# Sparse attention visits its sixteen token tiles alternately, most keys and fewest keys, instead of in rising order

## The reference, cut to what matters

```
# per block of 128 query tokens (start = 128 * t)
rel = relu(einsum('bqhd,bsd->bqhs', q_idx, k_idx)); score = einsum('bqhs,bqh->bqs', rel, w_idx)
score = where(key_pos <= qpos, score, -inf)
_, sel = top_k(score, 256)                      # an indexer picks 256 keys per query
kg, vg = gather(k, sel), gather(v, sel)
sc = einsum('bqkgd,bqjkd->bqkgj', qg, kg) * scale   # 8 heads, 2 key-value groups, head dim 64
p = softmax(where(valid, sc, -inf)); o = einsum('bqkgj,bqjkd->bqkgd', p, vg)
```

## Time and profile before

| what | value |
|---|---|
| median of 3 runs | 3377.59 us (3375.81 to 3380.34) |
| the profiled execution, its own time | 3379.56 us |
| its span (first to last instruction) | 3377.7 us, mean granted clock 0.97 |
| busy share of the span | PE 93%, PEld 78%, DVE 62%, ACT 54%, POOL 23% |
| sparse attention within the span | 1603.3 to about 2070 us |

### The profile page before, as it was taken

The page is one execution under the profiler, slowest core; times in us unless marked ns, Lnnn a source line. Parts: engine busy times, 40 slices in busy tenths (PEclk is TensorE's granted clock), DMA queues, the critical chain, the costliest instruction groups (busy, mean ns, idle before and its releaser), DMA issues. The chain is left out here.

```text
span 3377.7 us, 51228 instructions
## 1 busy us (share of the span) xinstructions
PE 3145.0 (93%) x17304; PEld 2641.0 (78%) x17304; DVE 2081.9 (62%) x5122; ACT 1822.9 (54%) x3613; POOL 776.7 (23%) x1078
## 2 busy tenths in 40 slices
PE   7999879999979999997899997999989999869998
PEld 5888768888868777776667776999878888769997
DVE  5767668888845666564899886534446666632112
ACT  5565556676756766663777774211246666632121
POOL 6444411011012122232211001101034444311110
PEclk8999989999989999998899998999999999979999
DMA  4666664436152222225511103544432222244332
GB/s 172 201 200 200 201 137 90 95 71 142 57 196 78 75 86 78 82 79 125 138 43 31 31 20 99 175 132 132 167 124 69 74 74 56 62 144 127 124 125 75
DMA packets 307188, 370.46 MB, mean 110 GB/s; under 512 B 24800, under 2 KB 251936, under 8 KB 303088
## 3 DMA queue, kind: packets, MB, share of 16 engines
q1 hardware_dynamic: 293728, 320.77, 32.7%
q0 software_dynamic: 13200, 46.42, 4.3%
HBM read 216.32 MB, written 150.80 MB: 109 GB/s over the span
## 5 line engine op out<-in xcount | busy, mean ns | idle before, releaser
L93 PE MATMUL i_p_g<-i_hT_lo,i_wh 128*128 128x512 f32 x768 | 308.2, 401 | 9.3 <-DVE i_wl L1639 9.3
L95 PE MATMUL i_p_g<-i_hT_hi,i_wh 128*128 128x512 f32 x768 | 306.0, 398 | 0.0
L94 PE MATMUL i_p_g<-i_hT_hi,i_wl 128*128 128x512 f32 x768 | 306.0, 398 | 0.0
L1657 DVE SCALAR_TENSOR_TENSOR i_score<-i_relu,i_w,i_score 128x1024 f32<-128x1024 f32 (+7 forms) x154 | 155.2, 1024 | 166.6 <-ACT i_relu L1542 164.7
L1552 ACT ACTIVATE i_above<-i_score,i_less 128x2048 bf16<-128x2048 f32 (+13 forms) x140 | 183.1, 1308 | 104.5 <-POOL i_less L1609 67.6
L1081 DVE TENSOR_TENSOR mla_tl<-mla_p_t,mla_th 128x512 fp32r<-128x512 f32 (+1 forms) x320 | 186.1, 606 | 45.3 <-ACT mla_th L1124 41.8
L1124 ACT ACTIVATE mla_th<-mla_p_t 128x512 fp32r<-128x512 f32 (+1 forms) x320 | 163.9, 530 | 86.4 <-PE mla_p_t L1021 83.8
L1081 DVE TENSOR_TENSOR dsa_tl<-dsa_p_t,dsa_th 128x512 fp32r<-128x512 f32 x272 | 180.0, 686 | 42.8 <-ACT dsa_th L1124 36.6
L1051 DVE CUSTOM_DVE_ANT_0 dsa_probs<-dsa_p_s,dsa_mask 128x512 f32<-128x512 f32 (+3 forms) x320 | 184.6, 605 | 16.0 <-PE dsa_p_s L1806 14.5
L1124 ACT ACTIVATE dsa_th<-dsa_p_t 128x512 fp32r<-128x512 f32 x272 | 155.4, 593 | 70.4 <-PE dsa_p_t L1021 69.7
L1542 ACT ACTIVATE i_relu<-i_p_s 128x1024 f32<-128x1024 f32 (+7 forms) x176 | 141.6, 813 | 77.8 <-DVE i_score L1654 39.4
(11 more groups left out here) (337 smaller groups left out, 9667.9 us busy)
## 6 DMA issues: line engine op xcount, KB each, us to landing
scratch_gates<-i_ob SPq DMA_DIRECT2D x95, 256.0 KB, 2.4
m_m<-scratch_gates SPq DMA_DIRECT2D x64, 256.0 KB, 4.0
f_hs<-scratch_h2T SPq DMA_DIRECT2D x16, 1024.0 KB, 9.9
scratch_qkT<-b_th SPq DMA_DIRECT2D x64, 192.0 KB, 2.6
scratch_qkT<-b_tl SPq DMA_DIRECT2D x64, 192.0 KB, 2.9
i_ws<-in_w_in SPq DMA_DIRECT2D x24, 512.0 KB, 4.4
b_xt<-in_x SPq DMA_DIRECT2D x16, 512.0 KB, 4.8
scratch_h<-b_xh POOLq DMA_DIRECT2D x16, 512.0 KB, 3.0
```

The lines of the kernel that those rows point to most:

```text
L93: pe.matmul(out, l[0], r[1], start=start, stop=False)
L94: pe.matmul(out, l[1], r[0], start=False, stop=False)
L95: return pe.matmul(out, l[0], r[0], start=False, stop=stop)
L1657: nc.vector.scalar_tensor_tensor(out=acc, in0=r, scalar=w[:, t, h:h + 1], in1=acc, op0=ALU.mult, op1=ALU.add).then_inc(summed, 1)
```

## The change

A list `order` of tiles replaces the rising order: 0, 1, 15, 2, 14, 3, 13, 4, 12, 5, 11, 6, 10, 7, 9, 8. Buffers, waits and loads now count places in this list (x), and tiles (t) only where the data are addressed. The wait for the second piece of keys and values moves to the third place, since tile 15 stands there. Every unit keeps its own work; what changes is which unit's blocks stand beside which unit's scores. The loops (k, k) for k = 1 to 16 and (2, 1) stay. The fourteen loops (k+1, k) for k = 2 to 15 go; in their place come seven loops of **many scores beside few blocks**, (16, 2), (15, 3), (14, 4), (13, 5), (12, 6), (11, 7), (10, 8), and seven of **few scores beside many blocks**, (3, 16), (4, 15), (5, 14), (6, 13), (7, 12), (8, 11), (9, 10). The blocks that stand alone at the end are those of tile 8, nine instead of 16.

```diff
+        few, many = list(range(2, NT // 2 + 1)), list(range(NT - 1, NT // 2, -1))
+        self.order = [0, 1] + [t for pair in zip(many, few) for t in pair]
         self.units = [dict(keys=[P * (t + 1)] * 4, blocks=[(j, 0) for j in range(t + 1)])
-                      for t in range(NT) for g in range(KV)]
+                      for t in self.order for g in range(KV)]
...
     def load(self, sp, n):
-        t, g = n // KV, n % KV
-        if t < 2 or g:
+        x, g = n // KV, n % KV
+        if x < 2 or g:
             return
-        if t == 2:
+        if x == 2:
             self.index_in.wait_mask(sp)
-        sp.wait_ge(self.sems["moved"], self.sems["n_s"][KV * (t - 1)])
-        self.load_queries(sp, t)
+        sp.wait_ge(self.sems["moved"], self.sems["n_s"][KV * (x - 1)])
+        self.load_queries(sp, x)
...
     def wait_scores(self, pe, n):
-        t = n // KV
-        pe.wait_ge(self.q_in[t % 2], 32 * (t // 2 + 1))
-        if n in (0, 4 * KV):
-            pe.wait_ge(self.kv_in[n // (4 * KV)], 16 * 5)
+        x = n // KV
+        pe.wait_ge(self.q_in[x % 2], 32 * (x // 2 + 1))
+        if n in (0, 2 * KV):
+            pe.wait_ge(self.kv_in[n // (2 * KV)], 16 * 5)
...
     def store(self, n):
-        t, g = n // KV, n % KV
+        t, g = self.order[n // KV], n % KV
```

More of the change, by code:

```diff
@@ L1767, in load, with load_queries @@
     def load(self, sp, n):
-        t, g = n // KV, n % KV
-        if t < 2 or g:
+        x, g = n // KV, n % KV
+        if x < 2 or g:
             return
-        if t == 2:
+        if x == 2:
             self.index_in.wait_mask(sp)
-        sp.wait_ge(self.sems["moved"], self.sems["n_s"][KV * (t - 1)])
-        self.load_queries(sp, t)
-    def load_queries(self, sp, t):
+        sp.wait_ge(self.sems["moved"], self.sems["n_s"][KV * (x - 1)])
+        self.load_queries(sp, x)
+    def load_queries(self, sp, x):
+        t = self.order[x]
         at, keys = slice(t * P, (t + 1) * P), P * (t + 1)
         for half in range(2):
-            sp.dma_start(self.q[half * HD:(half + 1) * HD, t % 2].bitcast(F32),
+            sp.dma_start(self.q[half * HD:(half + 1) * HD, x % 2].bitcast(F32),
                          self.qbT[half].rearrange("j (r d) t -> d (j r) t", d=HD)[:, :, at])\
-                .then_inc(self.q_in[t % 2], 16)
-        sp.dma_start(self.m[:, t % 2, 0:keys], self.mask[at, 0:keys]).then_inc(self.m_in[t % 2], 16)
+                .then_inc(self.q_in[x % 2], 16)
+        sp.dma_start(self.m[:, x % 2, 0:keys], self.mask[at, 0:keys]).then_inc(self.m_in[x % 2], 16)
     def wait_scores(self, pe, n):
-        t = n // KV
-        pe.wait_ge(self.q_in[t % 2], 32 * (t // 2 + 1))
-        if n in (0, 4 * KV):
-            pe.wait_ge(self.kv_in[n // (4 * KV)], 16 * 5)
+        x = n // KV
+        pe.wait_ge(self.q_in[x % 2], 32 * (x // 2 + 1))
+        if n in (0, 2 * KV):
+            pe.wait_ge(self.kv_in[n // (2 * KV)], 16 * 5)
     def wait_values(self, pe, n): ...
```

## The result

The changed kernel takes **3386.85 us** (median of 11 runs, 3385.14 to 3390.61); the kernel before, run beside it on the same chip, 3378.42 us (11 runs, 3375.81 to 3383.83). The ratio is 1.0023, with an interval of 1.0015 to 1.0032: 8.4 us slower by the medians, 5 to 11 us by the interval. Predicted were 3389, which is 11.2 us more.

A forecast was written before the change was run, and what follows sets the result against it. No engine alone was taken to bound sparse attention: DVE paces rows of chunks, PE rows of blocks, with waits behind exponentials. 49.3 - 31.8 - 6.3 = +11.2 us on 3377.59 gave 3389 us, range 3378 to 3399.

The forecast's parts named there:

- Step 1: Sparse attention: (3, 2) to (9, 8), 70.4 us, become (3, 16) to (9, 10), 119.7 us at PE's pace: +49.3 us.
- The waits of DVE, foretold as 0.2 to 0.3 before each block: In (3, 16) to (9, 10), DVE would idle 0.2 to 0.3 us before each L1081, with PE at 0.905 a block.
- Step 2: Sparse attention: (10, 9) to (16, 15), 136.6 us, become (10, 8) to (16, 2), 104.8 us at DVE's pace: -31.8 us.
- The waits of DVE, the unknown between 0 and 14.4 us: In (16, 2) to (10, 8), DVE waits behind an exponential once a loop at 1.2 us, 8.4 us together.
- under 13.5 would be A: Profile sign: (16, 2) to (10, 8) take 14 to 15.5 us each by DVE; under 13.5 would mean PE bounds them.
- Step 3: End of sparse attention: seven blocks fewer stand alone, at 0.905 us each: -6.3 us.
- (k, k) equal: The loops (k, k) and (2, 1), in both kernels, were taken as taking equal time.
- Rival A: Sparse attention: PE bounds all loops, so the 49 moved blocks cancel: -1.4 us, 3376.2; chance 0.2 with all up to +6.7.
- Rival B: TensorE's clock falls once in each of the seven large loops: +11 us on top, 3400; chance 0.15.
- Rival C: Tile 15's loads are late: a gap of a few us at 1621, 3392 to 3395; chance 0.05 with others.
- towards 80 us: Total wait of PE at L1805 for DVE to read a score bank would grow from 58 us towards 80.
- The stage's end: Sparse attention would end at about 2081 us instead of 2070, moving everything behind it.

The follow-up runs named there:

- the rising order with the lead by size: The kernel before with four chunks ahead of the blocks for units of up to eight chunks, eight for larger ones: 3375.47 us, ratio 0.9988.
- the falling order: The kernel before with tiles in the order 0, 1, 15, 14, down to 2: 3374.74 us, ratio 0.9988.
- the outward order: The changed kernel with its pairs in opposite order, 0, 1, 8, 9, 7, 10, up to 2, 15: 3395.86 us, ratio 1.0043.

## Why the prediction was right

- **Step 1, the small loops (+49.3): right.** Predicted 119.7 us for the new seven, measured 118.9; +48.5. A unit of few scores costs its (a, a) and then 0.905 us for every further block. The closeness is partly luck: the (5, 5) of the kernel before, read into the 119.7, held a fall of the clock, 1.6 us, and so did the (5, 4) in the 70.4 that went; without that last one the step is +50.1. That it is PE's 0.905 is shown by the pair of experiments: 0.22 us of transposes in each block cost 0.20 us, a memset on DVE next to nothing. The waits of DVE, foretold as 0.2 to 0.3 before each block, are 0.21 before eleven of sixteen in (3, 16).
- **Step 2, the large loops (-31.8): right, 2.8 us too small.** They took 103.0 us, where 104.8 were predicted and 92.3 would be PE's; those they replace took 137.6 by DVE's chunks, where 136.6 was read by spreads; together -34.6. The waits of DVE, the unknown between 0 and 14.4 us, were put at 8.4 and are 6.9. They are not one per loop at 1.2: (16, 2) has a single 0.24, (12, 6) two that add up to 2.03. That DVE sets the pace is shown by the second pair of experiments: 11 us more for PE moved these loops by nothing, and some 6.8 us more for DVE by 4.6, the rest going into its waits. The sign "under 13.5 would be A" was a bad one: three of the seven are under it by the distance of spreads, (16, 2), (15, 3) and (14, 4), because the spread comes early there, and not because PE sets the pace.
- **Step 3, the end (-6.3): the mis-sized term, -8.6 measured.** Seven lone blocks are 6.3 of it. The rest are the two things that the prediction left standing: PE's wait for the last exponential is 1.92 us and was 2.67, and the clock did not fall behind it, which is worth 1.6. PE's first lone block and two stretches at this place of the kernel after, with the columns of the earlier trace rows:

```profile
2064.20 0.65 PE L1021 MATMUL dsa_p_t<-ident,dsa_probs 128*128 128x128 f32 x4 [1.92 <-ACT dsa_probs L1116]
...
2062.60:2066.00 3.40, 1.80 (x12) 1.60 (x13) 0.77 (x2) 2.35 (x5) 0.00 (x0) 1.00 0.00 0
2066.00:2069.40 3.40, 3.40 (x25) 2.91 (x23) 3.06 (x7) 2.19 (x4) 0.61 (x1) 1.00 0.02 5
```

PE was idle for 1.92 us before 2064.20 and the clock stayed at 1.00; before, it was idle for 2.67 us, and 0.51 followed. Neither is a rule: behind the same idle of 1.92 us it fell in the profile with DVE's memset in the loops of few scores, at 2063.4, and behind 2.67 us it stayed at 1.00 in the rising order with the lead by size.

- **(k, k) equal: nearly.** Those that moved are (5, 5), by 1.6 us, because the clock fell there before (in both profiles) and not after, and (3, 3), by 0.6. The sum of the terms as measured is 48.5 - 34.6 - 8.6 - 0.8 = +4.5 in the two profiles, where +11.2 was said; by the medians it is +8.4. Without the falls of the clock on either side the terms are 50.1 - 34.6 - 7.0 + 0.6, some +9, which is nearer to what the forecast priced, work without luck. The 4 us between the stage and the medians are not all explained: 2.9 of them are in stretches that the change does not touch, where the stage's beginning alone lies anywhere from 1605.4 to 1610.7 us in the profiles of this case, and the profiled execution of the kernel before is itself 1.1 us above its median. How often the clock falls in the executions without a profile stays open.
- **Rival A** (PE bounds all loops, 3376) is refuted by the time, by 103.0 us against its 92.3 and by PE's added work in the large loops, which cost nothing. **Rival B** (the clock falls in the large loops) did not occur as priced: the one fall behind the stage's beginning is at 1763.4, where (14, 4) ends and (14, 14) starts, and (14, 14) took 22.12 us instead of the 21.93 of before. But its place recurs. In the six profiles of this case that pair unlike sizes with a lead of eight, the clock falls nine times ahead of the end, each time within 2.2 us of where a loop of many scores beside few blocks ends; in the three of the falling order it never does. So such a loop, in which PE waits often, seems to bring a fall, though not each time and cheaply here, since DVE sets the pace of the eight chunks that follow; which waits bring it is not shown. The Trainium skill, TensorE: Matmul & The Clock Gate, section A second HAM failure mode: psum-queue depth-cycling, tells of another kernel in which micro-idles of PE between groups of matmuls make the clock swing; inside (16, 2), where PE's weight loads fill 7.25 of 13.6 us and wait 12 times for DVE, it keeps 1.00. **Rival C** did not occur: 0.24 us at 1623.56.
- **Foretold and wrong:** the total wait of PE for a score bank, "towards 80 us", is 65.4. (16, 2) has 5.2 us of it and (3, 16) 0.6, but the loops that went had some as well, 2.8 in (16, 15) and 1.6 in (9, 8). The prediction counted what came and not what left. The stage's end was foretold 11 us later and came 6.4 later in the profile, 1.8 of it by a later beginning.

## What to carry to other kernels

Where two kinds of work are interleaved and each is bound by another engine, put units beside each other that have about as much of the one as of the other: an unlike neighbour leaves one engine idle in one loop, and that time is not given back in full in the next, since there the other engine is at its own pace. End with the smallest unit, since its part alone is what nothing covers; the falling order did that with one unlike pair instead of seven, and gained 0.1% on the rising one; a lead by the size of the unit gained as much by itself. Before such a change, take each loop's time as the longest of each engine's own pace, add the waits that the order of its steps brings, and sum over the loops, not over the stage: the busy shares hardly see the order, PE 93% and DVE 62% of the span in the rising, the alternate, the outward and the falling one.

## What the runs showed of the hardware

- A DVE operation's duration in the trace is not what it adds. The memset of 128x128 shows as 0.165 us and moved the next chunk by 0.11 on average; the 128x512 chunk shows as 0.685 and starts 0.61 apart. Read prices from the distance of starts. The Trainium skill, VectorE: DVE Perf Modes, says in Two Vector instructions with no wait between them that a held instruction starts only when every earlier Vector instruction has finished. These chunks start 0.07 us before the row of the one ahead ends, so by that page they are not held.
- TensorE's granted clock fell to 0.5, the 1.2 GHz level, for 3.4 or 6.8 us at a time. A fall cost about 1.6 us among blocks, where PE sets the pace, and 0.2 us at the start of (14, 14), where DVE does. Its places partly recurred ((5, 5) and the end in both profiles of before) and partly did not ((5, 4) in one). The changed kernel had one in the stage behind its beginning, the outward order five, the three profiles of the falling order none; that the falling order prevents them is not shown, since the rising order with the lead by size had none either.
- The longest stretch at the lower level lies where the stage begins, in the profile of the kernel after and both of the kernel before. The stretch of the kernel after (columns of the earlier trace rows):

```profile
1592.80:1620.10 27.30, 11.75 (x52) 10.80 (x53) 9.12 (x51) 10.43 (x33) 0.89 (x2) 0.50 0.86 209
```

Of the kernel before it lasted 20.5 us in one profile and 27.3 in the other, for the same program. It reaches into the stage's first loops: (2, 1) took 4.91 us where it was short, and 5.56 in the two profiles where it was long.
